# Attention blocks in pairs of heads, with score products alternating between two 64-row halves and maxima negated where they are taken

## The chip, the cores and the metric

The kernel runs on one core of a Trainium2 chip. The metric is the time of one execution on the device in microseconds (us), as the median of several runs; the kernel before takes 3290.98 us (three runs, 3290.24 to 3291.83).

## The reference, cut to what matters

Two transformer-like blocks on a sequence of 1024 rows and a width of 1024, all in float32. The change touches only the attention of the second block, which has 8 heads of 64 channels. It mixes three dilated windows, and each branch normalises itself and is weighted by its softmax denominator:

```
for window, dilation in ((128, 1), (512, 4), (2048, 16)):
    s = einsum(q, k) * HEAD_DIM ** -0.5 - slopes * dist      # causal, masked
    m = max(s); p = exp(s - m); denom = sum(p)
    o = einsum(p, v) / denom;  lse = m + log(denom)
    ...
w = softmax(stack(lses));  o = einsum(w, stack(outs))
```

Because the three weights are the denominators, the mixture equals one causal softmax over all keys, in which a key counts once for each window that reaches it. So the kernel adds to each score a bias (the slope term, the logarithm of that count, and -1e30 where no window reaches) and computes one softmax for each head and each block of 128 queries. Beside it, on the other 512 channels, runs a state-space mixer (S5) of 32 groups of 16 channels.

## The kernel before, in words

The program is written out by hand for five engines, with semaphores between them; nothing reorders it. The big matrix products around the attention are split into high and low parts (lines 125 to 127) and fill most of the span. Between them lies the attention stage, which `att_pe`, `att_act` and `att_dve` write out for TensorE, ScalarE and VectorE.

A *block* n is one head h and one group of 128 queries i; there are 64. Its keys are the first (i + 1) * 128 rows, and its width is counted here in units of 128, k = i + 1, from 1 to 8. Before, n runs through the eight i of a head and then goes to the next head. A block passes through these stations:

- scores (PE, line 1631): one or two products of 64 rows of `QK` into two PSUM banks, chosen by n % 2. Head h uses rows 0 to 63 of the array if h is even, and rows 64 to 127 if it is odd. `scores(n)` waits until the maximum of block n - 2 is taken, since that frees the banks.
- maximum (DVE, line 1728): a custom instruction adds the bias, writes the sum to `sco` and gives its maximum; its second part reads out the accumulator. Line 1733 then multiplies the maximum by -1.
- exponential (ACT, line 1695) with that value as its bias, and the sum of the row as a by-product.
- transposes (PE, line 1641), k of them, into two banks; copy out (ACT, line 1685).
- values (PE, line 1651), k products of 64 columns.
- finish (DVE, lines 1738 and 1741): reciprocal of the sum, and scaling of the result from PSUM.

The engines go in steps n. PE: `scores(n + 2)`, `transposes(n)`, a piece of the state-space mixer, `values(n - 1)`. DVE: `finish(n - 2)`, `maximum(n + 1)`, a piece of the mixer. ACT: exponential of n, copy of n - 1, a piece of the mixer. The mixer's piece is s = n % 8, and it isn't changed. On DVE the pieces are: s0, s2 and s3 short; s4, s5, s6 and s7 long (tables for the next groups, and in s5 and s6 the scan). On PE, s5 waits for the first part of the scan and s7 for the second. GpSimd makes tables and stores at its own pace. The bias of a head (`head_bias`, line 1714) is made from two tables that are built in three cuts during the first head (`bias_dve`, lines 1608 to 1620), and lies in one of two slots, h % 2.

Of the kernel before, what the change touches and what calls it, by code (L numbers as in the profile page):

```python
# [5 lines left out]
P = 128  # L6
S = 1024
D = 1024
NT = S // P
# [34 lines left out]
def program(nc, x, p, stream, cols, rows, gate_mats, pool_mats, inv_count, ssm_g, ssm_bc, x_mid, out):  # L44
# [7 lines left out]
    with ctx:  # L52
# [1512 lines left out]
        def glu_dve(dve):  # L1565
# [32 lines left out]
        at_s, at_m, at_n, at_e, at_tr, at_pt, at_pv, at_r, at_o = (sem(f"at_{s}") for s in (  # L1598
            "s", "m", "n", "e", "tr", "pt", "pv", "r", "o"))
# [22 lines left out]
        def att_pe(pe):  # L1622
            def scores(n):
                h, i = divmod(n, NT)
                rows_ = slice(64 * (h % 2), 64 * (h % 2) + 64)
                W = (i + 1) * P
                if n >= 2:
                    pe.wait_ge(at_m, n - 1)
                for c0 in range(0, W, HALF):
                    w = min(HALF, W - c0)  # L1630
                    last = nc.tensor.matmul(ps[:, 2 * (n % 2) + c0 // HALF, 0:w], QK[rows_, h // 2, i * P:(i + 1) * P],  # L1631
                                            QK[rows_, 4 + h // 2, c0:c0 + w], start=True, stop=True)
                last.then_inc(at_s, 1)

            def transposes(n):
                i = n % NT
                pe.wait_ge(at_e, n + 1)
                if n:
                    pe.wait_ge(at_pt, n)
                for k in range(i + 1):  # L1640
                    last = nc.tensor.transpose(ps[:, 4 + k // 4, (k % 4) * P:(k % 4 + 1) * P],  # L1641
                                               prob[:, n % 2, k * P:(k + 1) * P], ident[:, :])
                last.then_inc(at_tr, 1)

            def values(n):
                h, i = divmod(n, NT)
                pe.wait_ge(at_pt, n + 1)
# [8 lines left out]
            pe.wait_ge(u_out, GT)  # L1656
            scores(0)
            scores(1)
# [19 lines left out]
        def att_act(act):  # L1678
            def rest(n):
                i = n % NT  # L1680
                act.wait_ge(at_tr, n + 1)
# [8 lines left out]
            for n in range(NA):  # L1690
                w = (n % NT + 1) * P
                act.wait_ge(at_n, n + 1)
                if n >= 2:
                    act.wait_ge(at_tr, n - 1)
                nc.scalar.activation(prob[:, n % 2, 0:w], sco[:, n % 2, 0:w], ACT.Exp, bias=nm_[:, n:n + 1],
                                     accum_out=den_[:, n:n + 1]).then_inc(at_e, 1)
# [13 lines left out]
        def att_dve(dve):  # L1710
# [8 lines left out]
            def maximum(n, made):  # L1719
                h, i = divmod(n, NT)  # L1720
                w = (i + 1) * P
# [3 lines left out]
                if n >= 2:  # L1725
# [3 lines left out]
                                               in0=ps[:, b:b + 2, :].rearrange("p a b -> p (a b)")[:, 0:w],  # L1729
                                               in1=bias_h[:, h % 2, S - w:S], scale=1.0, scalar=-3e38, op0=ALU.add,  # L1730
                                               op1=ALU.max, accum_out=mx_[:, n:n + 1]).then_inc(at_m, 1)
                dve.wait_ge(at_m, n + 1)
                nc.vector.tensor_scalar(nm_[:, n:n + 1], mx_[:, n:n + 1], -1.0, None, ALU.mult).then_inc(at_n, 1)

            def finish(n):
                h, i = divmod(n, NT)
                dve.wait_ge(at_e, n + 1)
# [9 lines left out]
            bias_dve(dve, near)  # L1747
            made = [head_bias(0, near)]
            maximum(0, made[0])
            for n in range(NA):  # L1750
                if n % NT == 0:
                    prepare = ssm_prepare_dve(dve, n // NT + 1) if n // NT + 1 < NB else iter(())
                if n == 1 or n == 3:
                    dve.wait_ge(dve_chain, made[0])
                if n >= 2:
                    finish(n - 2)
                if n + 1 < NA:
                    maximum(n + 1, made[(n + 1) // NT])
                if n == 0:
                    dve.wait_ge(io_done, 2)  # L1760
                    bias_dve(dve, middle)
                    made[0] = head_bias(0, middle)
                if n == 2:
                    bias_dve(dve, far)
                    made[0] = head_bias(0, far)
# [459 lines left out]
```

## Time and profile before

| | |
|---|---|
| median of 3 runs | 3290.98 us (3290.24 to 3291.83) |
| profiled execution | 3291.88 us, of it 3290.1 us span |
| PE busy over the span | 3130.1 us (95%) |
| DVE busy | 1519.9 us (46%) |
| ACT busy | 878.3 us (27%) |
| attention stage, from the first maximum to the last finish | about 2098.5 to 2386.0 us |

The span is the time from the first to the last instruction of the profiled execution. Busy shares are means over the whole program, in which the attention stage is less than a tenth; what bounds the stage has to be read from its own stretch. PE's granted clock has two levels, and the profile gives it as a share of 2.4 GHz (1.00 is 2.4 GHz, 0.50 is 1.2 GHz).

### The profile page before, as it was taken

How to read it: one execution, taken by the hardware profiler on the slowest of the kernel's cores; microseconds unless marked ns; L12 is line 12 of the kernel's file. 1: busy time of each engine (PE TensorE's matmuls, PEld its weight loads, DVE VectorE, ACT ScalarE, POOL GpSimd, SP SyncE). 2: the span in 40 equal slices, each digit the busy share in tenths (PEclk: the TensorE clock that was granted, in tenths of full speed). 3: DMA queues.
4: the chain of work that ended last, by engine and by line, in shares of the span. 5: the costliest groups of instructions: out<-in, count | busy, mean ns of one | idle time of the engine just before them, and what ended most of it. 6: DMA issues, size and time to landing. Idle time of an engine off the chain costs nothing.

```text
span 3290.1 us, 36983 instructions
## 1 busy us (share of the span) xinstructions
PE 3130.1 (95%) x14151; PEld 2557.6 (78%) x14151; DVE 1519.9 (46%) x2478; ACT 878.3 (27%) x1323; POOL 172.2 (5%) x372
## 2 busy tenths in 40 slices
PE   7999999999999899999999999899989999999997
PEld 5777888888877678888888778676767788888885
DVE  5654444444454533333333553688745233333335
ACT  5523222221123331111111341145444211111112
POOL 0000000000000000000000001244201000000001
PEclk9999999999999999999999999799989999999998
DMA  3121111111111121111111321000023111111112
GB/s 120 39 80 65 54 51 51 51 45 45 39 51 39 52 77 58 52 38 47 62 45 38 115 90 52 2 5 7 5 77 115 52 51 39 45 61 48 38 51 115
DMA packets 50394, 178.15 MB, mean 54 GB/s; under 512 B 6656, under 2 KB 7424, under 8 KB 50160
## 3 DMA queue, kind: packets, MB, share of 16 engines
q1 hardware_dynamic: 37440, 136.33, 12.3%
q0 software_dynamic: 12848, 40.38, 3.4%
q8 instruction: 70, 1.15, 0.1%
q14 instruction: 36, 0.29, 0.0%
HBM read 158.73 MB, written 16.78 MB: 53 GB/s over the span
## 4 chain that ended last, share of the span: by engine, by line
PE 87%; DVE 8%; ACT 2%; issue 2%; DMA 1%; SPq 0%; DVEq 0%; POOL 0%; ACTq 0%
PE ps L125 27%; PE ps L127 27%; PE ps L126 27%; PE ps L1631 1%; PE ps L261 1%; PE ps L1651 1%; DVE acc L810 1%; DVE sco L1728 1%; DVE region_b L120 1%; DVE acc L176 1%; DVE acc L184 1%; PE ps L1641 0%; ACT region_b L116 0%; PE ps L1454 0%; DMA raw<-stream 0%
## 5 line engine op out<-in xcount | busy, mean ns | idle before, releaser
L125 PE MATMUL ps<-region_a,region_b 128*128 128x512 f32 x1664 | 658.2, 396 | 19.4 <-DVE region_a L220 9.8
L127 PE MATMUL ps<-region_a,region_b 128*128 128x512 f32 x1664 | 650.2, 391 | 0.0
L126 PE MATMUL ps<-region_a,region_b 128*128 128x512 f32 x1664 | 650.2, 391 | 0.0
L810 DVE TENSOR_TENSOR acc<-acc,ps 128x1024 f32<-128x1024 f32 x288 | 351.0, 1220 | 330.3 <-PE ps L127 330.3
L125 PE MATMUL ps<-region_b,region_a 128*128 128x512 f32 x1088 | 431.8, 397 | 17.8 <-DVE region_b L120 10.4
L126 PE MATMUL ps<-region_b,region_a 128*128 128x512 f32 x1088 | 427.9, 393 | 0.0
L127 PE MATMUL ps<-region_b,region_a 128*128 128x512 f32 x1088 | 427.9, 393 | 0.0
L120 DVE TENSOR_TENSOR region_b<-raw,region_b 128x1024 fp32r<-128x1024 f32 x176 | 212.4, 1223 | 390.3 <-ACT region_b L116 390.2
L125 PEld LDWEIGHTS ps<-region_a,region_b 128*128 128x128 f32 x1664 | 314.5, 189 | 87.7 <-issue 10.0
L126 PEld LDWEIGHTS ps<-region_a,region_b 128*128 128x128 f32 x1664 | 314.6, 189 | 65.3 <-issue 1.7
L127 PEld LDWEIGHTS ps<-region_a,region_b 128*128 128x128 f32 x1664 | 314.0, 189 | 66.1
L125 PE MATMUL ps<-region_b 128*128 128x512 f32 x896 | 350.8, 392 | 4.2 <-DVE acc L810 2.8
L127 PE MATMUL ps<-region_b 128*128 128x512 f32 x896 | 348.8, 389 | 0.0
L126 PE MATMUL ps<-region_b 128*128 128x512 f32 x896 | 348.7, 389 | 0.0
L125 PEld LDWEIGHTS ps<-region_b,region_a 128*128 128x128 f32 x1088 | 215.3, 198 | 61.3 <-issue 10.1
L725 ACT ACTIVATE rtmp<-ps 128x512 f32<-128x512 f32 x88 | 52.7, 598 | 735.9 <-PE ps L127 735.9
L127 PEld LDWEIGHTS ps<-region_b,region_a 128*128 128x128 f32 x1088 | 215.1, 198 | 41.1
L126 PEld LDWEIGHTS ps<-region_b,region_a 128*128 128x128 f32 x1088 | 215.3, 198 | 39.4
L116 ACT ACTIVATE region_b<-raw 128x1024 fp32r<-128x1024 f32 x176 | 181.5, 1050 | 161.5 <-DMA raw<-stream 132.0
L120 DVE TENSOR_TENSOR region_a<-raw,region_a 128x1024 fp32r<-128x1024 f32 x74 | 89.5, 1224 | 262.2 <-ACT region_a L116 262.2
L125 PEld LDWEIGHTS ps<-region_b 128*128 128x128 f32 x896 | 168.2, 188 | 40.7 <-DVE acc L810 4.0
L127 PEld LDWEIGHTS ps<-region_b 128*128 128x128 f32 x896 | 168.2, 188 | 35.2
(289 smaller groups left out, 3337.2 us busy)
## 6 DMA issues: line engine op xcount, KB each, us to landing
raw<-stream SPq DMA_DIRECT2D x252, 512.0 KB, 3.2
x_mid<-acc POOLq DMA_DIRECT2D x24, 512.0 KB, 3.1
acc<-x SPq DMA_DIRECT2D x8, 512.0 KB, 8.3
rold<-x POOLq DMA_DIRECT2D x16, 256.0 KB, 3.5
old_a<-x_mid POOLq DMA_DIRECT2D x8, 512.0 KB, 9.5
old_b<-x_mid POOLq DMA_DIRECT2D x8, 512.0 KB, 7.8
out<-acc POOLq DMA_DIRECT2D x8, 512.0 KB, 2.9
old_s<-x_mid POOLq DMA_DIRECT2D x6, 512.0 KB, 5.6
```

Source lines behind the costliest of these rows:

```text
L116: nc.scalar.activation(slot[:, 0, :], raw[:, odd, :], ACT.Copy).then_inc(hi_done, 1)
L120: nc.vector.tensor_tensor(slot[:, 1, :], raw[:, odd, :], slot[:, 0, :].bitcast(f32), ALU.subtract).then_inc(unit_ready, 1)
L125: nc.tensor.matmul(psum, lhs(0), rhs(0), start=first, stop=False)
L126: nc.tensor.matmul(psum, lhs(0), rhs(1), start=False, stop=False)
L127: return nc.tensor.matmul(psum, lhs(1), rhs(0), start=False, stop=last)
L176: nc.vector.scalar_tensor_tensor(out=acc[:, t, :], in0=acc[:, t, :], scalar=rinv_post[:, t:t + 1], in1=gb[:, N.post, :], op0=ALU.mult, op1 ...
L184: nc.vector.scalar_tensor_tensor(out=a, in0=a, scalar=N.factor, in1=N.old(t), op0=ALU.mult, op1=ALU.add).then_inc(N.sem["res"], 1)
L261: last = nc.tensor.transpose(ps[:, 6 + d % 2, t * P:(t + 1) * P], xn[:, t, d * P:(d + 1) * P], ident[:, :])
L725: nc.scalar.activation(rtmp[:, half, :], ps[:, up_bank(c, j, half), :], ACT.Silu).then_inc(F.sem["ge"], 1)
L810: nc.vector.tensor_tensor(acc[:, t, :], acc[:, t, :], src, ALU.add).then_inc(F.sem["de"], 1)
L1631: last = nc.tensor.matmul(ps[:, 2 * (n % 2) + c0 // HALF, 0:w], QK[rows_, h // 2, i * P:(i + 1) * P], QK[rows_, 4 + h // 2, c0:c0 + w], st ...
L1651: last = nc.tensor.matmul(ps[:, 6, 0:HEAD_DIM], probT[:, n % 2, k, :], V[:, k, h * HEAD_DIM:(h + 1) * HEAD_DIM], start=k == 0, stop=k == i)
```

## The change

Blocks are numbered so that two heads, 2p and 2p + 1, run together: n = 16p + 2i + (h % 2). The widths k then go 1, 1, 2, 2, up to 8, 8 in sixteen steps, where before they went 1 to 8 in eight steps. The mixer's pieces stay at n % 8. The scores of both blocks of a pair are issued together, at the even step before, and their products alternate between the two halves of the rows and go to different banks. Before it issues a pair, PE waits for both maxima of the pair before. The instruction for the maximum now multiplies the sum of scores and bias by -1 and takes the minimum, so that its result is the negated maximum; line 1733 is gone, and the exponential uses a scale of -1. The tables of the bias are built at other steps, for two heads at once.

```diff
-        mx_, nm_, den_, rd_ = (stats[:, i, :] for i in range(4))
+        _, nm_, den_, rd_ = (stats[:, i, :] for i in range(4))
+        def block_of(n):
+            pair, r = divmod(n, 2 * NT)
+            return 2 * pair + r % 2, r // 2
...
-            def scores(n):
-                h, i = divmod(n, NT)
-                rows_ = slice(64 * (h % 2), 64 * (h % 2) + 64)
+            def scores_pair(m):
+                h, i = block_of(2 * m)
                 W = (i + 1) * P
-                if n >= 2:
-                    pe.wait_ge(at_m, n - 1)
+                if m:
+                    pe.wait_ge(at_m, 2 * m)
                 for c0 in range(0, W, HALF):
                     w = min(HALF, W - c0)
-                    last = nc.tensor.matmul(ps[:, 2 * (n % 2) + c0 // HALF, 0:w], QK[rows_, h // 2, i * P:(i + 1) * P],
-                                            QK[rows_, 4 + h // 2, c0:c0 + w], start=True, stop=True)
-                last.then_inc(at_s, 1)
+                    for r in range(2):
+                        rows_ = slice(64 * r, 64 * r + 64)
+                        last = nc.tensor.matmul(ps[:, 2 * r + c0 // HALF, 0:w], QK[rows_, h // 2, i * P:(i + 1) * P],
+                                                QK[rows_, 4 + h // 2, c0:c0 + w], start=True, stop=True)
+                        if c0 + w == W:
+                            last.then_inc(at_s, 1)
...
             for n in range(NA):
-                if n + 2 < NA:
-                    scores(n + 2)
+                if n % 2 == 0 and n + 2 < NA:
+                    scores_pair(n // 2 + 1)
...
-                act.wait_ge(at_n, n + 1)
+                act.wait_ge(at_m, n + 1)
...
-                                               in1=bias_h[:, h % 2, S - w:S], scale=1.0, scalar=-3e38, op0=ALU.add,
-                                               op1=ALU.max, accum_out=mx_[:, n:n + 1]).then_inc(at_m, 1)
-                dve.wait_ge(at_m, n + 1)
-                nc.vector.tensor_scalar(nm_[:, n:n + 1], mx_[:, n:n + 1], -1.0, None, ALU.mult).then_inc(at_n, 1)
+                                               in1=bias_h[:, h % 2, S - w:S], scale=-1.0, scalar=3e38, op0=ALU.add,
+                                               op1=ALU.min, accum_out=nm_[:, n:n + 1]).then_inc(at_m, 1)
...
-                if n == 4:
-                    made.append(head_bias(1))
-                if n % NT == NT - 1 and n // NT + 2 < N_HEADS:
-                    made.append(head_bias(n // NT + 2))
+                if n % (2 * NT) >= 2 * NT - 3 and len(made) < N_HEADS and n % (2 * NT) < 2 * NT - 1:
+                    dve.wait_ge(at_m, n + 2)
+                    made.append(head_bias(len(made)))
```

On TensorE, in the second head of the kernel before, step 12 and the beginning of 13 (`qk` are the scores, `prob` the transposes, `ztb`, `zs` and `ub` the mixer, `probT` the values):

```order
L1631 MATMUL ps<-qk 128x512 [waits at_m]
L1631 MATMUL ps<-qk 128x384
L1641 MATMUL ps<-ident,prob 128x128 [waits at_pt,at_e]
L1641 MATMUL ps<-ident,prob 128x128 x4
L1447 MATMUL ps<-ztb 128x128 [waits s5_cp]
L1447 MATMUL ps<-ztb 128x128 x3
L1651 MATMUL ps<-v,probT 128x64 [waits at_o,at_pt]
L1651 MATMUL ps<-v,probT 128x64 x3
L1631 MATMUL ps<-qk 128x512 [waits at_m]
L1631 MATMUL ps<-qk 128x512
```

On TensorE, after the change, steps 10 and 11, with pieces s2 and s3 of the mixer:

```order
L1637 MATMUL ps<-qk 128x512 [waits at_m]
L1637 MATMUL ps<-qk 128x512
L1637 MATMUL ps<-qk 128x384 x2
L1648 MATMUL ps<-ident,prob 128x128 [waits at_pt,at_e]
L1648 MATMUL ps<-ident,prob 128x128 x5
L1442 MATMUL ps<-ident,zs 128x128 [waits s5_cp]
L1442 MATMUL ps<-ident,zs 128x128 x3
L1658 MATMUL ps<-v,probT 128x64 [waits at_o,at_pt]
L1658 MATMUL ps<-v,probT 128x64 x4
L1648 MATMUL ps<-ident,prob 128x128 [waits at_pt,at_e]
L1648 MATMUL ps<-ident,prob 128x128 x5
L1442 MATMUL ps<-ident,ub 128x128 [waits ub_made,s5_cp]
```

Scores no longer come at every step: twice as many come at every second one, ahead of both steps' transposes, and only their first product waits.

On VectorE, in the second head of the kernel before, step 13 (the block of width 7, then the scan's first part, which is piece s5):

```order
L1738 RECIPROCAL stats<-stats 128x1 [waits at_e]
L1741 TENSOR_SCALAR att_o<-ps,stats 128x64 [waits at_pv,at_r]
L1728 ISA sco,stats<-ps,bias_h 128x896 [waits at_e,at_s]
L1728 ISA stats 128x1
L1733 TENSOR_SCALAR stats<-stats 128x1 [waits at_m]
L1373 TENSOR_TENSOR m1b<-ps,cs 128x512 [waits s5_s]
```

On VectorE, after the change, step 13 (the first of the two blocks of width 8, the bias of the next pair's first head, then the scan's first part):

```order
L1742 RECIPROCAL stats<-stats 128x1 [waits at_e]
L1745 TENSOR_SCALAR att_o<-ps,stats 128x64 [waits at_pv,at_r]
L1734 ISA sco,stats<-ps,bias_h 128x1024 [waits at_e,at_s]
L1734 ISA stats 128x1
L1720 SCALAR_TENSOR_TENSOR bias_h<-dist,lmul 128x1024 [waits at_m]
L1373 TENSOR_TENSOR m1b<-ps,cs 128x512 [waits s5_s]
```

The multiplication by -1 is gone, and the bias of a later head has moved ahead of the scan.

## Rows read from the trace of the kernel before

**Rows 1.** Windows: length, busy time and instructions by engine, granted clock, DMA.

```profile
2098.50:2147.20 48.70, 45.53 (x178) 32.20 (x178) 42.18 (x150) 17.90 (x34) 6.98 (x18) 0.60 0.02 4
2215.40:2249.50 34.10, 31.26 (x193) 24.19 (x192) 30.48 (x122) 16.87 (x32) 15.05 (x36) 0.95 0.03 5
2351.90:2386.00 34.10, 31.11 (x204) 24.87 (x202) 14.50 (x51) 16.83 (x31) 4.03 (x8) 0.95 0.03 6
```

**Rows 2.** Timeline of VectorE, third head: start, length, instruction, idle time before.

```profile
2192.61 0.28 DVE L1741 TENSOR_SCALAR att_o<-ps,stats 128x64 f32<-128x64 f32 x1 [0.65 <-PE ps L1651]
2192.81 0.95 DVE L1728 CUSTOM_DVE_ANT_0 sco<-ps,bias_h 128x768 f32<-128x768 f32 x1
...
2193.87 0.28 DVE L1298 TENSOR_TENSOR tmp_v<-z,st 128x128 f32<-128x128 f32 x1
...
2197.86 1.08 DVE L1728 CUSTOM_DVE_ANT_0 sco<-ps,bias_h 128x896 f32<-128x896 f32 x1
2198.86 0.08 DVE L1728 DVE_READ_ACCUMULATOR2_ANT stats<- 128x1 f32 x1
2198.98 0.15 DVE L1733 TENSOR_SCALAR stats<-stats 128x1 f32<-128x1 f32 x1
2199.05 0.68 DVE L1373 TENSOR_TENSOR m1b<-ps,cs 128x512 f32<-128x512 f32 x1
```

**Rows 3.** Timeline of ScalarE, the exponential of the same block.

```profile
2199.17 1.04 ACT L1695 ACTIVATE prob<-sco,stats 128x896 f32<-128x896 f32 x1 [3.02 <-DVE stats L1733]
```

**Rows 4.** Windows of VectorE's pieces s0, s2, s3, s4, s5, s6, bias, s7.

```profile
2182.38:2184.29 1.91, 1.91 (x19) 1.69 (x16) 1.84 (x9) 1.23 (x4) 1.83 (x6) 1.00 0.00 0
2187.90:2189.16 1.26, 1.26 (x13) 1.17 (x11) 1.23 (x4) 1.15 (x4) 1.26 (x2) 1.00 0.00 0
2190.61:2191.79 1.18, 1.18 (x12) 1.01 (x10) 1.11 (x7) 1.06 (x3) 0.98 (x4) 1.00 0.05 14
2193.87:2197.46 3.59, 3.59 (x25) 2.84 (x24) 3.49 (x13) 2.16 (x4) 1.36 (x3) 1.00 0.08 15
2199.05:2202.82 3.77, 3.32 (x27) 2.90 (x26) 3.46 (x29) 1.83 (x3) 0.00 (x0) 1.00 0.01 2
2204.54:2209.77 5.23, 2.94 (x18) 2.29 (x18) 5.06 (x15) 2.04 (x3) 0.00 (x0) 0.89 0.00 0
2210.57:2211.70 1.13, 1.13 (x8) 1.13 (x7) 1.13 (x2) 1.01 (x3) 0.00 (x0) 0.50 0.00 0
2211.70:2215.55 3.85, 3.85 (x29) 3.33 (x28) 3.71 (x14) 3.55 (x4) 2.04 (x5) 0.95 0.00 0
```

**Rows 5.** Chain of waits in order of time: start, length, instructions.

```profile
2181.85 0.98 PE ps L1430 x8
2182.83 1.93 PE ps L1651 x16
2184.76 1.05 PE ps L1631 x2
...
2186.18 0.44 PE ps L1442 x4
...
2188.06 0.48 PE ps L1641 x3
...
2191.88 0.63 PE ps L1651 x6
...
2364.89 0.70 PE ps L1641 x5
2365.59 0.89 PE ps L1447 x8
...
2367.32 1.91 PE ps L1631 x4
```

**Rows 6.** Windows around the scan of the third head.

```profile
2204.00:2208.00 4.00, 2.66 (x19) 1.98 (x18) 3.86 (x10) 2.04 (x3) 0.00 (x0) 1.00 0.00 0
2208.00:2212.00 4.00, 3.05 (x14) 3.08 (x15) 3.86 (x16) 1.31 (x3) 0.00 (x0) 0.58 0.01 4
```

More of the change, by code:

```diff
@@ L1595, in program @@
         stats = at("stats", OFF_B + 31 * KB, [4, N_HEADS * NT])
-        mx_, nm_, den_, rd_ = (stats[:, i, :] for i in range(4))
+        _, nm_, den_, rd_ = (stats[:, i, :] for i in range(4))
         io_done = sem("io_done")
-        at_s, at_m, at_n, at_e, at_tr, at_pt, at_pv, at_r, at_o = (sem(f"at_{s}") for s in (
-            "s", "m", "n", "e", "tr", "pt", "pv", "r", "o"))
+        at_s, at_m, at_e, at_tr, at_pt, at_pv, at_r, at_o = (sem(f"at_{s}") for s in (
+            "s", "m", "e", "tr", "pt", "pv", "r", "o"))
         ot_tr, ot_hi, ot_lo = sem("ot_tr"), sem("ot_hi"), sem("ot_lo")
         NA = N_HEADS * NT
+        def block_of(n):
+            pair, r = divmod(n, 2 * NT)
+            return 2 * pair + r % 2, r // 2
         def bias_dve(dve, cut):
@@ L1656, in att_pe @@
             pe.wait_ge(u_out, GT)
-            scores(0)
-            scores(1)
+            scores_pair(0)
             for n in range(NA):
-                if n + 2 < NA:
-                    scores(n + 2)
+                if n % 2 == 0 and n + 2 < NA:
+                    scores_pair(n // 2 + 1)
                 transposes(n)
@@ L1690, in att_act @@
             for n in range(NA):
-                w = (n % NT + 1) * P
-                act.wait_ge(at_n, n + 1)
+                w = (block_of(n)[1] + 1) * P
+                act.wait_ge(at_m, n + 1)
                 if n >= 2:
                     act.wait_ge(at_tr, n - 1)
-                nc.scalar.activation(prob[:, n % 2, 0:w], sco[:, n % 2, 0:w], ACT.Exp, bias=nm_[:, n:n + 1],
+                nc.scalar.activation(prob[:, n % 2, 0:w], sco[:, n % 2, 0:w], ACT.Exp, bias=nm_[:, n:n + 1], scale=-1.0,
                                      accum_out=den_[:, n:n + 1]).then_inc(at_e, 1)
@@ L1747, in att_dve @@
             bias_dve(dve, near)
-            made = [head_bias(0, near)]
+            made = [head_bias(h, near) for h in range(2)]
             maximum(0, made[0])
@@ L1752, in att_dve @@
                     prepare = ssm_prepare_dve(dve, n // NT + 1) if n // NT + 1 < NB else iter(())
-                if n == 1 or n == 3:
-                    dve.wait_ge(dve_chain, made[0])
+                if n == 3 or n == 7:
+                    dve.wait_ge(dve_chain, made[1])
                 if n >= 2:
@@ L1757, in att_dve @@
                 if n + 1 < NA:
-                    maximum(n + 1, made[(n + 1) // NT])
-                if n == 0:
+                    maximum(n + 1, made[block_of(n + 1)[0]])
+                if n == 1:
                     dve.wait_ge(io_done, 2)
                     bias_dve(dve, middle)
-                    made[0] = head_bias(0, middle)
-                if n == 2:
+                    made = [head_bias(h, middle) for h in range(2)]
+                if n == 4:
                     bias_dve(dve, far)
-                    made[0] = head_bias(0, far)
-                if n == 4:
-                    made.append(head_bias(1))
-                if n % NT == NT - 1 and n // NT + 2 < N_HEADS:
-                    made.append(head_bias(n // NT + 2))
+                    made = [head_bias(h, far) for h in range(2)]
+                if n % (2 * NT) >= 2 * NT - 3 and len(made) < N_HEADS and n % (2 * NT) < 2 * NT - 1:
+                    dve.wait_ge(at_m, n + 2)
+                    made.append(head_bias(len(made)))
                 ssm_step_dve(dve, n, prepare)
```

10 lines of the change are left out of this document (5 added, 5 removed).

## The prediction

> **What bounds the kernel now.** I read first the windows of the attention stage, head by head, since the change touches nothing else. The first head takes longer (48.7 us); from the second on each head takes 34.1 us, with PE busy for 31.3 and DVE for 30.5 [rows 1]. Neither engine is full, so next I read DVE's timeline for what it waits for. Its pieces of the mixer are 1.91 + 1.26 + 1.18 + 3.59 + 3.77 + 5.23 + 3.85 = 20.8 us in a head, and the bias of a later head 1.13 [rows 4]. A maximum with its negation, from its start to the next instruction's, takes 1.06 us at width 6 and 1.19 at width 7 [rows 2], so 0.26 + 0.133k; over k = 1 to 8 that is 6.9 us. A finish is 0.40 (from the end of piece s4 at 2197.46 to the maximum at 2197.86) [rows 2, 4], eight are 3.2. Sum: 32.0 us of the 34.1. The remaining 2 us are waits for PE's values in the light steps; the row with 0.65 us is one [rows 2]. In the steps with s4 to s7 DVE is late, and PE waits: of 8 us around the scan it is busy for 5.7, and its granted clock falls to 0.58 in the second half, which is a stretch at the lower level (1.2 GHz) inside one at 2.4 [rows 6].
>
> So a head is: DVE late in four steps, PE late in the others. PE runs up to two blocks of scores ahead, and this slack couples the two only loosely. The last head shows PE alone: DVE is busy for 14.5 us there and the head still takes about 34 [rows 1].
>
> **Prices of PE's parts**, from one view at full clock [rows 5]: scores 1.05 us at width 4 and 1.91 at width 8, so 0.2 to begin and 0.213k; each product of 512 columns is two MATMULs of 0.43. Transposes 0.48 at 3 and 0.70 at 5: 0.15 + 0.11k. Values 0.63 at 3 and 1.93 at 8: 0.22k or a little more. Mixer: s0 0.98, s1 to s3 0.44 each, s4 and s5 0.89 each (8 instructions), s7 has 24 such instructions, 2.7.
>
> **The change, part by part.**
>
> Negation: 64 instructions leave DVE. The readout starts at 2198.86 and the next instruction after the negation at 2199.05 [rows 2]; without the negation it can follow some 0.06 later, so it saves 0.13 (bounds 0.07 and 0.19). That is 2.1 us in a pair of heads, 8.3 in all, on DVE. The exponential begins 0.31 after the readout [rows 2, 3] and can begin about 0.17 earlier. A maximum now costs 0.13 + 0.133k, and DVE's work for two heads is 61.9 us where it was 64.
>
> Pairing of products: before, adjacent score products use the same rows, so the trace shows no case of two halves side by side. Bounds: each of the extra changes of half costs like a beginning (0.2 us for 12 products more, +2.4 us for two heads), or all passes of one half hide under the other, so that a pair of width k costs 0.2 + 0.213k where two cost 0.4 + 0.427k. A product is two MATMULs that go in order; with alternating products the second of one half lies beside the first of the other, but the two of one half don't lie side by side. So I take a middle: of four passes three remain up to width 4 (0.2 + 0.32k), and five of eight at width 8 (2.35). The Trainium skill, "TensorEngine Tiling (Array Packing)", Key Properties and Theoretical Speedup, says that tiles work in parallel and up to twice as fast, which is the lower of the two bounds. Its PSUM Bottleneck speaks against the change: the evacuation isn't sped up; the rows agree, for DVE holds the heavy steps.
>
> The new wait: PE's scores at an even step n now wait for the maximum of block n + 1, which DVE takes in the same step n, behind `finish(n - 2)`, which waits for `values(n - 2)`, the last thing PE did. Before, PE needed only the maximum of block n, taken a step earlier. So at each of 31 pairs PE stops for at least: values to finish 0.10, finish to maximum 0.20 (2192.61 to 2192.81) [rows 2, 5], the maximum itself 0.133k + 0.08, and some 0.07 to PE. Queued behind the wait are the transposes of n, whose exponential is ready long since, the mixer and the values, for which DVE's next finish waits. Nothing can be carried over from one pair to the next: each round lasts as long as the slower of the two.
>
> A round, from the moment that the second maximum of the pair of width k is taken. PE: 0.07, scores of width k + 1, transposes, piece, values of the block before; then transposes, piece, values; then 0.30 and the maximum. DVE: piece, finish, maximum of the next, piece, finish, maximum; its first finish can't begin before PE's first values are done. The longest path:
> - k = 1 (s0, s1): PE, 0.9 + 0.26 + 0.98 + 1.93, then 0.26 + 0.44 + 0.2, 0.3 + 0.4: 5.7
> - k = 2 (s2, s3): PE to the first values 2.4 (with 0.2 for a copy of the mixer), then DVE 0.3 + 0.4 + 1.18 + 0.4 + 0.4: 5.1
> - k = 3 (s4, s5): DVE, 3.6 + 3.8 + 0.8 + 1.3: 9.5
> - k = 4 (s6, s7): DVE, 5.2 + 3.9 + 0.8 + 1.6: 11.5
> - k = 5 (s0, s1): PE, 2.0 + 0.7 + 1.0 + 0.8, then 0.7 + 0.4 + 1.1, 0.3 + 0.9: 7.9
> - k = 6 (s2, s3): PE, 2.2 + 0.8 + 0.4 + 1.1, then 0.8 + 0.4 + 1.2, 0.3 + 1.1: 8.4
> - k = 7 (s4, s5): PE to the first values 5.5 (2.4 + 0.9 + 0.9 + 1.2); DVE had ended s4 at 3.6 and stood; then DVE 0.3 + 1.2 + bias 1.1 + 3.8 + 0.4 + 1.2: 13.5
> - k = 8 (s6, s7): DVE with the second bias, 1.1 + 5.2 + 3.9 + 0.8 + 0.5: 11.5
>
> Sum 73.1 us for two heads, where it was 68.2: +4.9. The cause is an uneven match: light pieces now fall to the narrow pair and again to the widths 5 and 6, where PE is long and DVE stands (about 3 us each), and DVE can't use that later.
>
> Over the stage: the second and third pair of heads +4.9 each. In the last pair no tables are made in its second half; k = 7 becomes 11.5 and k = 8 about 11, so +2.5. In the first pair the building of the bias (48.7 - 34.1 = 14.6 us more) stays on DVE, but now lies in steps with narrow blocks; PE, at the low clock in much of that window (0.60) [rows 1], has less to do there. I count +3. Sum 15.3.
>
> The clock: after k = 4 PE has finished at about 7.9 of 11.5 and stands 3.6 us, longer than the stretch before the fall of rows 6; after k = 8 it stands twice, 1.2 and 1.4, much as in rows 6. Before, the slow stretch lay under DVE's tables (s7). Now it falls into k = 5 and k = 1, which are PE's. A stretch at half rate costs half of its length; from the window at 0.58, in which some 3.4 us are at the lower level, I take 1.7 for k = 5 and 1 for k = 1, and three pairs of heads to pay it: +8.
>
> The rest of the program is the same, instruction by instruction. Total +23 us: 3291.9 in the profiled execution gives 3314.9; on the median of 3291.0 that is 3314.
>
> **Rivals.**
>
> The halves don't overlap. Then the scores of k + 1 cost 0.2 + 0.427(k + 1), and the rounds come to 6.0, 5.5, 9.6, 11.5, 8.9, 9.6, 14.7, 11.5, sum 77.3. Against 73.1 that is +4.2 in each of four, +17 over the forecast: 3331. For it: no row shows an overlap. Against it: nothing in the program keeps the halves apart, since their banks and rows differ.
>
> The halves overlap fully, and the clock costs nothing. The rounds sum to 71.4, +3.2 for two heads: +3.2 twice, +1 and +1 for the others, so about +8: 3299. For it: the skill's rule and the few low stretches before.
>
> The clock stays low through the light rounds. At half rate PE's parts of k = 1, 2, 5 and 6 (21 us without the stall) cost up to 20 more for two heads; with half of that in each of three pairs, +30 over the forecast's terms without the clock: 3336. For it: the first head at 0.60. Against it: every other head regains 1.00 within 4 us.
>
> Faster: the lock-step costs nothing, because PE's stall lies beside DVE's pieces everywhere. Then DVE's work decides, 61.9 us for two heads, -6.3 each, -25: 3266. It needs PE's rounds k = 1, 2, 5, 6, 7 to be shorter than DVE's; they would have to lose 3 us each at the widths 5 and 6, so my prices of PE would be off by a third. At half of that it's -12: 3279. The negation alone would take this direction.
>
> **How the numbers follow.** Forecast 0.49, of itself 3305 to 3324; no overlap 0.15; full overlap 0.14; low clock 0.11; faster 0.11. A measurement of this kernel tells about 0.2% (6.6 us) from no change. From full overlap I give half to "same" and a little of the forecast's lower edge: same 0.10, faster 0.10, slower 0.80. The range cuts part of the faster case below and of the low clock above: 3287 to 3340.
>
> **What would show it.** Two heads take about 73 us, three times alike, with rounds in which DVE waits about 3 us for values at the widths 5 to 7. PE's longest idle times end at the maximum's readout ahead of each pair of scores. DVE's busy time in the stage falls by some 8 us. Score MATMULs of the two halves start closer together than 0.43 us if they overlap. The granted clock dips after the widths 4 and 8. I'm wrong if two heads take under 68 us, or if PE doesn't wait at the scores; or if the time comes from outside the stage.

## The result, and the profile after

The changed kernel takes 3329.34 us (median of 4, 3326.83 to 3331.08), against 3291.4 of the kernel before on the same chip: a ratio of 1.0114, 95% interval 1.0101 to 1.0126. It is slower by 38 us; the forecast was 23, and the range 3287 to 3340 holds the time. The profiled execution has a span of 3325.0 us, where it was 3290.1 (+34.9); it is the fastest of the four, so its parts add up to some 3 us less than the medians. The attention stage alone has grown by that much, as the windows of its four pairs of heads show (the columns are those of [rows 1]; the same cuts of the kernel before are 82.8, 68.2, 68.4 and 68.1 us long, 287.5 in all):

```profile
2096.71:2190.05 93.34, 65.72 (x368) 52.37 (x368) 69.64 (x257) 35.30 (x66) 21.56 (x53) 0.71 0.02 4
2190.05:2264.21 74.16, 59.22 (x384) 50.03 (x384) 58.11 (x227) 34.78 (x64) 29.02 (x71) 0.84 0.02 5
2264.21:2342.71 78.50, 61.54 (x384) 50.72 (x384) 58.68 (x228) 34.77 (x64) 29.31 (x71) 0.80 0.02 5
2342.71:2418.80 76.09, 59.26 (x396) 48.42 (x396) 41.70 (x157) 34.36 (x62) 16.36 (x37) 0.87 0.02 5
```

The pairs cost 10.5, 6.0, 10.1 and 8.0 us more. From the second pair on neither PE nor DVE is busy for more than about four fifths of it, and the granted clock is 0.80 to 0.87, where [rows 1] has 0.95. So both engines stand in turn. The view of waits over the stage says for what (engine, line, what it waited for: us in total, times, longest):

```profile
DVE att_o L1745 <- PE ps L1658: 70.7, 37, 7.3
PEld ps L1637 <- DVE stats L1734: 64.5, 31, 12.8
PE ps L1637 <- DVE stats L1734: 59.7, 31, 12.6
```

In the kernel before the same view has

```profile
DVE att_o L1741 <- PE ps L1651: 36.8, 33, 4.8
PE ps L1631 <- DVE stats L1728: 11.9, 2, 11.7
```

PE now stops ahead of each of the 31 later pairs of scores, for 48 us more than before: that is the lock-step. DVE waits 34 us more for values; e2 below has nearly the same without the lock-step, so these waits come from the new order of the blocks as well.

The negation is gone as meant. In VectorE's timeline [rows 2] had the readout, the multiplication, and then the mixer's first instruction 0.19 us after the readout; now the mixer starts with the readout:

```profile
2198.21 0.55 DVE L1734 CUSTOM_DVE_ANT_0 sco<-ps,bias_h 128x384 f32<-128x384 f32 x1
2198.68 0.08 DVE L1734 DVE_READ_ACCUMULATOR2_ANT stats<- 128x1 f32 x1
2198.68 0.33 DVE L1298 TENSOR_TENSOR tmp_v<-z,st 128x64 f32<-128x64 f32 x1
```

DVE's busy time fell from 1519.9 to 1509.1 us. And the halves overlap, more than forecast. In the chain of waits, pairs of scores of widths 6, 7 and 8 (each two blocks):

```profile
2221.50 1.56 PE ps L1637 x8
...
2229.15 1.77 PE ps L1637 x8
...
2237.14 1.99 PE ps L1637 x8
```

One block alone took 1.05 at width 4 and 1.91 at width 8 [rows 5]. Two blocks of width 8 now take 1.99, and the three rows give 0.27 + 0.213k for a pair: the second half costs nothing but 0.1 us. By line and form over the stage, the 96 MATMULs of 512 columns show the same: together they keep PE busy for 34.3 us, where it was 57.4. The mean of one record (813 ns; 694 before) doesn't tell the overlap, and it is raised by the lower clock here; in e3, with a stage clock like that of the kernel before (0.88 and 0.89), it is 653 ns:

```profile
L1637 PE MATMUL ps<-qk 64*128 64x512 f32 x96 | 34.3, 813 | 32.4 <-DVE stats L1734 32.4
```

The clock is the rest. Around width 8 of the second pair of heads, windows of 4 us:

```profile
2248.00:2252.00 4.00, 2.41 (x12) 2.00 (x12) 3.41 (x12) 1.19 (x2) 0.00 (x0) 0.50 0.01 2
2252.00:2256.00 4.00, 4.00 (x22) 4.00 (x21) 3.90 (x9) 1.08 (x2) 0.00 (x0) 0.50 0.00 0
2256.00:2260.00 4.00, 4.00 (x20) 4.00 (x21) 3.83 (x20) 2.06 (x4) 0.00 (x0) 0.50 0.00 0
2260.00:2264.00 4.00, 3.90 (x32) 3.76 (x30) 1.61 (x6) 2.40 (x3) 1.68 (x7) 0.89 0.00 0
```

Ahead of them PE had stood for 2.68 us, waiting for the scan. The clock fell in the 3.6 us of work behind that (0.80 in the window 2246 to 2248, 0.50 in the next), and then PE stood for another 1.59 us for the maximum:

```profile
2245.67 1.16 PE L1447 MATMUL ps<-ztb 128*128 128x128 f32 x8 [2.68 <-DVE m1b L1373]
2246.67 2.58 PE L1658 MATMUL ps<-v,probT 128*128 128x64 f32 x14
2250.83 0.58 PE L1637 MATMUL ps<-qk 64*128 64x128 f32 x2 [1.59 <-DVE stats L1734]
```

The clock is then at 1.2 GHz until about 2261, and PE is the late engine there. The chain (start, length) and then DVE's timeline:

```profile
2251.63 1.90 PE ps L1648 x8
2253.53 2.88 PE ps L1658 x14
2256.41 1.71 PE ps L1648 x8
2258.12 0.43 PE ps L1454 x2
```

```profile
2261.52 0.16 DVE L1742 RECIPROCAL stats<-stats 128x1 f32<-128x1 f32 x1
2264.01 0.28 DVE L1745 TENSOR_SCALAR att_o<-ps,stats 128x64 f32<-128x64 f32 x1 [2.33 <-PE ps L1658]
```

DVE is ready at 2261.68 and can begin at 2264.01, when PE is done with the values. Two MATMULs of s7 take 0.22 us at 2.4 GHz and 0.43 here.

Of the runs below, e3 had two disturbed executions among its ten (3985 and 12186 us), which are left out of its median; the texts that were written ahead of later runs quote 3297.8 us, the median with them.

### The profile page after: what moved, and what is told of

It is laid out like the page before. It is cut to its first block, busy times and chain, and to the rows that moved or that the text cites. A ratio compares the mean times of both kernels' runs of the same rounds, so it can differ in the third digit from the quotient of the medians.

```text
span 3325.0 us, 36922 instructions
## 1 busy us (share of the span) xinstructions
PE 3112.9 (94%) x14151; PEld 2559.6 (77%) x14151; DVE 1509.1 (45%) x2416; ACT 881.5 (27%) x1323; POOL 169.8 (5%) x372
## 4 chain that ended last, share of the span: by engine, by line
PE 88%; DVE 8%; ACT 2%; issue 2%; DMA 0%; SPq 0%; DVEq 0%; POOL 0%; ACTq 0%
PE ps L125 27%; PE ps L127 27%; PE ps L126 27%; PE ps L1658 2%; PE ps L261 1%; DVE sco L1734 1%; PE ps L1637 1%; PE ps L1648 1%; DVE acc L810 1%; DVE region_b L120 1%; DVE acc L176 0%; DVE acc L184 0%; PE ps L1447 0%; ACT region_b L116 0%; DVE region_a L220 0%
## 5 line engine op out<-in xcount | busy, mean ns | idle before, releaser
L125 PEld LDWEIGHTS ps<-region_b,region_a 128*128 128x128 f32 x1088 | 215.1, 198 | 60.9 <-issue 10.1
```

Of the source, the lines that this page charges most:

```text
L125: nc.tensor.matmul(psum, lhs(0), rhs(0), start=first, stop=False)
```

## The experiments

All times are medians with the 95% interval of the ratio to the kernel before, which ran beside them (3291.4 to 3292.5 us).

**e1: the negation alone.** The kernel before, with the maximum taken negated.

```diff
-                act.wait_ge(at_n, n + 1)
+                act.wait_ge(at_m, n + 1)
...
-                                               op1=ALU.max, accum_out=mx_[:, n:n + 1]).then_inc(at_m, 1)
-                dve.wait_ge(at_m, n + 1)
-                nc.vector.tensor_scalar(nm_[:, n:n + 1], mx_[:, n:n + 1], -1.0, None, ALU.mult).then_inc(at_n, 1)
+                                               op1=ALU.min, accum_out=nm_[:, n:n + 1]).then_inc(at_m, 1)
```

> The kernel before with the second part of the change alone: the instruction for the maximum gives the negated maximum, the 64 multiplications by -1 are gone, the blocks keep their order and their single scores. Theory (DVE holds the steps with s4 to s7, PE the others): a head loses 0.13 us in each of the 4 to 8 steps in which DVE is late, 34.1 becomes 33.1 to 33.6, so 4 to 8 us in all: 3283 to 3287. Rival (the negation lies in DVE's free time, or PE decides everywhere): 3290 to 3292, heads of 34.1.

Measured: 3288.7 us, ratio 0.9990 (0.9981 to 0.9999). The negation brings 3.5 us, less than half of what it takes off DVE. DVE's waits for values grew instead:

```profile
DVE att_o L1739 <- PE ps L1651: 43.5, 32, 5.0
```

They were 36.8, so 6.7 of the freed time is spent waiting: DVE is late in part of the steps only.

**e2: pairs of heads without the paired scores.** The order of blocks after the change, but each block's scores issued by themselves at each step, with the old wait for block n - 2.

```diff
-                if n % 2 == 0 and n + 2 < NA:
-                    scores_pair(n // 2 + 1)
+                if n + 2 < NA:
+                    scores(n + 2)
```

> The changed kernel with its order of blocks and its negation, but scores issued singly at each step, two blocks ahead, after the maximum of block n alone, as before the change. Nothing of two halves lies side by side any more. Theory (the wait for both maxima ahead of a pair of scores costs more than the overlap gives): PE's idle time ahead of scores (124 us after the change) falls below 30; the scores of two heads cost about 9 us more PE time; rounds by the slower of PE and DVE sum to about 69.5 for two heads plus the low clock, so 3305 to 3318. Rival (the overlap is what keeps the changed kernel from being worse, and the order of the widths against the mixer's pieces is the loss): 3329 or slower, up to 3350.

Measured: 3312.47 us, ratio 1.0054 (1.0039 to 1.0070). Without the lock-step PE waits at the scores only once, for the bias of the first head; the same MATMULs, one after the other, cost 24 us more of PE than in pairs. DVE's waits for values stay at 66.3 us:

```profile
DVE att_o L1744 <- PE ps L1656: 66.3, 38, 7.4
```

```profile
L1636 PE MATMUL ps<-qk 64*128 64x512 f32 x96 | 58.6, 707 | 0.0
L1636 PE MATMUL ps<-qk 64*128 64x256 f32 x32 | 11.3, 437 | 12.4 <-DVE stats L1733 12.4
```

So the order in pairs of heads alone costs about 24 us (3312.5 against 3288.7 of e1), and issuing the scores as pairs at the even step adds 17 more, although it saves PE 39 us of products (92.6 us over all widths here, 53.9 after the change).

**e3: the pairs of scores behind the values.** The changed kernel with one call moved, so that PE does the values of n - 1 before it waits for the maxima.

```diff
-                if n % 2 == 0 and n + 2 < NA:
-                    scores_pair(n // 2 + 1)
                 transposes(n)
                 ssm_step_pe(pe, n)
                 if n:
                     values(n - 1)
+                if n % 2 == 0 and n + 2 < NA:
+                    scores_pair(n // 2 + 1)
```

> The changed kernel with one move: at an even step PE issues the next pair of scores after the transposes, the mixer's piece and the values of that step, not ahead of them. Same wait, same products. Theory (the wait blocks work that is ready): the stall of 0.5 us and the maximum's length at each of 31 pairs lies beside transposes and values; rounds of widths 1, 2, 5, 6 lose about 1 us each, 7 some 0.5 to 1, two heads take 67 to 72 instead of 74 to 78: 3300 to 3315. Rival (the wait only changes sides, DVE now stands for scores at odd steps): within 5 us of 3329.

Measured: 3296.4 us, the median of its eight undisturbed runs (3294.0 to 3300.4), ratio 1.0014 (1.0004 to 1.0024). The place of the wait is worth 33 of the 38 us. The waits at the scores have gone, and DVE's for values are back where they were:

```profile
L1637 PE MATMUL ps<-qk 64*128 64x512 f32 x96 | 27.0, 653 | 0.0
```

```profile
DVE att_o L1745 <- PE ps L1658: 34.3, 30, 5.1
```

**e4: the clock kept up.** The changed kernel, with products that nobody reads issued ahead of those scores and transposes at which PE would stand (16 products of 384 columns in 16 steps).

```diff
+            def filler(n, count):
+                if n and count:
+                    pe.wait_ge(at_pt, n)
+                    for _ in range(count):
+                        nc.tensor.matmul(ps[:, 4, 0:HALF - P], QK[:, 0, 0:P], QK[:, 4, 0:HALF - P], start=True, stop=True)
...
+                filler(n, {6: 4, 8: 4, 14: 2, 0: 1}.get(n % 16, 0))
                 if n % 2 == 0 and n + 2 < NA:
                     scores_pair(n // 2 + 1)
+                filler(n, {5: 1, 13: 3, 15: 1}.get(n % 16, 0))
                 transposes(n)
```

> The changed kernel with products that nobody reads, of 384 columns on all 128 rows (about 0.64 us each at full clock), put on PE where the trace after the change shows it standing for 1 to 4 us: four ahead of the scores at steps 6 and 8 of each sixteen, two at 14, one at 0, and one, three and one ahead of the transposes at steps 5, 13 and 15. 16 in each pair of heads, some 10 us of PE time added. Theory of the clock (PE at 1.2 GHz after its stalls is what the prediction sized too small): the granted clock of the stage rises towards 1.00, the last round of two heads goes from 14.7 to about 12, the fifth from 10.3 to 7.5 where it was that long, two heads take 71 to 73, so 3310 to 3320. Rival (the clock is only a symptom under waits that last anyway): the added work shows, 3329 to 3340.

Measured: 3316.59 us, ratio 1.0071 (1.0055 to 1.0086): 12.8 us less than the changed kernel, with work added. The second pair of heads:

```profile
2191.00:2262.76 71.76, 60.31 (x416) 46.30 (x416) 58.85 (x227) 34.88 (x65) 30.32 (x71) 1.00 0.03 5
```

At 2.4 GHz throughout it takes 71.8 us (the third 71.8 too), where the changed kernel had 74.2 and 78.5. Its first pair of heads takes 90.1, at a granted clock that is still 0.79.

**e5: the halves not side by side.** The changed kernel, with all products of one half first, then a product of 16 columns over all rows, then the other half.

```diff
-                for c0 in range(0, W, HALF):
-                    w = min(HALF, W - c0)
-                    for r in range(2):
-                        rows_ = slice(64 * r, 64 * r + 64)
+                for r in range(2):
+                    rows_ = slice(64 * r, 64 * r + 64)
+                    if r:
+                        nc.tensor.matmul(ps[:, 2, 0:16], QK[:, 0, 0:P], QK[:, 4, 0:16], start=True, stop=True)
+                    for c0 in range(0, W, HALF):
+                        w = min(HALF, W - c0)
```

> The changed kernel with the same wait and the same pairs, but all products of the lower half first, then one product of 16 columns on all 128 rows (its result is overwritten), then all of the upper half, so that no two halves lie side by side. Theory (alternating halves run fully beside each other; the trace after the change has 1.77 us for eight MATMULs of a pair of width 7 where two single blocks of before have 3.4): a pair of width 7 takes about 3.4 to 3.5 us again, two heads get about 6 us longer, 3329 becomes 3345 to 3357. Rival (the halves overlap little, and the shorter span of the scores in the trace is how MATMUL ends are modelled): within 5 us of 3329.

Measured: 3444.95 us, ratio 1.0463 (1.0447 to 1.0479), far above what either theory gave. The same stretch of the stage, of e5 and of the changed kernel:

```profile
2100.00:2380.00 280.00, 238.05 (x990) 177.60 (x990) 157.38 (x611) 88.91 (x170) 72.30 (x177) 0.63 0.02 3
```

```profile
2100.00:2380.00 280.00, 211.49 (x1295) 171.90 (x1293) 212.57 (x814) 119.74 (x224) 91.60 (x218) 0.79 0.02 5
```

PE is busier and does less: the granted clock is 0.63, mostly the level of 1.2 GHz. The cost of the products can't be told from the cost of the clock in this run.

**e6: the negation with other places for the tables.** e1, with one part of the next groups' tables on DVE in nearly each step. The numbers are how many parts DVE makes in the steps s0 to s7.

```diff
-        S5_PIECES = (1, 0, 0, 1, 2, 2, 1, 2)
+        S5_PIECES = (1, 1, 1, 2, 1, 1, 1, 1)
```

> The kernel before with the negation taken in the maximum (as in the first experiment, 3288.7 us), and VectorE's nine pieces that prepare the mixer spread 1, 1, 1, 2, 1, 1, 1, 1 over the eight steps of a head in place of 1, 0, 0, 1, 2, 2, 1, 2. Theory (a head is the sum over steps of the slower engine, and DVE stands in the light steps while it is late in s4 to s7): some 2 us a head move from late steps into DVE's idle time, 33.4 becomes 31.5 to 32.5, so 8 to 15 us: 3273 to 3281. Rival (PE alone needs the time, as in the last head): 3287 to 3290.

Measured: 3298.09 us, ratio 1.0018 (1.0009 to 1.0027): 9 us slower than e1, where the theory had it faster. The part now in s1 is six instructions, and each lasts as long as one of GpSimd's beside it. DVE's timeline, then GpSimd's:

```profile
2183.76 0.65 DVE L1299 TENSOR_TENSOR tmp_v<-zs,st 128x64 f32<-128x64 f32 x1
2184.33 0.65 DVE L1300 TENSOR_TENSOR tmp_v<-zs,st 128x64 f32<-128x64 f32 x1
```

```profile
2183.71 0.61 POOL L1299 TENSOR_TENSOR tmp_p<-vs,st 128x256 f32<-128x256 f32 x1
2184.29 0.61 POOL L1300 TENSOR_TENSOR tmp_p<-vs,st 128x256 f32<-128x256 f32 x1
```

The six take 3.6 us in this place (2183.48 to 2187.04).

**e7: e3 with the same places.**

```diff
-        S5_PIECES = (1, 0, 0, 1, 2, 2, 1, 2)
+        S5_PIECES = (1, 1, 1, 2, 1, 1, 1, 1)
```

> The changed kernel with the scores issued after the values (third experiment, 3297.8 us) and the same spreading 1, 1, 1, 2, 1, 1, 1, 1 of the mixer's pieces. Theory (what is left of the loss is the match of light pieces with PE's long rounds and of heavy pieces with DVE's): rounds 3, 4, 7 and 8 lose 1.5 to 2.5 us each and the light ones grow by less, two heads go from 69 or 70 to 63 to 66: 3275 to 3288. Rival (the rounds are bound by the chain scores, maximum, exponential, transposes and not by the pieces): 3294 to 3300.

Measured: 3306.98 us, ratio 1.0044 (1.0031 to 1.0058), 11 us slower than e3. Moving the parts costs about as much in both orders of blocks. Here too the time is lost where s1 falls: in the second pair of heads the rounds of the widths 1 and 5 (s0 and s1) take 7.7 and 10.3 us, 4.2 and 5.9 in e3, and the heavy round of width 7 gains 3.5. That GpSimd is the cause in this run wasn't looked at.

**e8: the negation, no part in s1.** e1 with

```diff
-        S5_PIECES = (1, 0, 0, 1, 2, 2, 1, 2)
+        S5_PIECES = (1, 0, 1, 2, 1, 2, 1, 1)
```

> The kernel before with the negation in the maximum and the mixer's pieces spread 1, 0, 1, 2, 1, 2, 1, 1. Step s1 gets none, where the sixth experiment lost: there six VectorE instructions of 64 columns took 0.35 to 0.78 us beside GpSimd's tables, 3.4 us together, where the same piece takes 1.2 at s3. Theory (VectorE's short instructions are slowed while GpSimd works in s0 and s1): away from it the spreading gains, a head takes 31.8 to 33 instead of 33.4, 3276 to 3286. Rival (light steps have no free time at all for more of it): 3288 to 3298.

Measured: 3281.52 us, ratio 0.9971 (0.9959 to 0.9983), 17 us faster than e6, from which it differs by one part fewer in s1 and one more in s5; the parts between move by a step. The six instructions that e6 has in s1 stand in s2 here, beside the end of GpSimd's tables, and take 1.4 us (2181.23 to 2182.65) in place of 3.6. Four of them run at 0.20 each within one of GpSimd's, which is the one held: it has 1.24 us in place of the 0.73 to 0.76 of its like. The fifth then lasts until about its end:

```profile
2181.50 0.20 DVE L1300 TENSOR_TENSOR tmp_v<-zs,st 128x64 f32<-128x64 f32 x1
...
2181.88 0.64 DVE L1302 TENSOR_TENSOR z<-tmp_v 128x64 f32<-128x64 f32 x1
```

```profile
2181.19 1.24 POOL L1303 TENSOR_TENSOR vs<-tmp_p 128x256 f32<-128x256 f32 x1
```

So the two seem to take turns. From the maximum of width 3 to that of width 4, e6 takes 1.9 to 2.6 us more than e8 in each of six heads and 1.1 in the first, 15 us in all; that is the price of the place. Beside it, two heads of e6 lose another 2.8 us each between the maxima of widths 6 and 7, with the granted clock down. The second head, of e6 and of e8:

```profile
2139.06:2176.03 36.97, 34.34 (x195) 26.07 (x194) 31.38 (x116) 17.08 (x32) 15.99 (x35) 0.86 0.03 5
2139.01:2170.95 31.94, 29.54 (x195) 22.66 (x194) 29.72 (x116) 16.95 (x32) 15.66 (x35) 1.00 0.03 6
```

Other steps give back some of it; the profiled spans differ by 13 us. The Trainium skill, "GPSIMD Engine Reference", Key points, says that GpSimd shares its SBUF interfaces with VectorE, with contention for instructions of two SBUF inputs. These have two, and the trace agrees; its price here is up to a factor of three.

**e9: the negation, with two parts in s4 and s7.** e8 with

```diff
-        S5_PIECES = (1, 0, 1, 2, 1, 2, 1, 1)
+        S5_PIECES = (1, 0, 1, 1, 2, 1, 1, 2)
```

> As the run before it, but 1, 0, 1, 1, 2, 1, 1, 2: step s3 gets the third piece (1.4 us), not the third and the fourth (3.6). Theory: s3 now stays within PE's time of that step (about 3 us), s5 loses 1.4, a head takes 32 to 33: 3277 to 3286. Rival as there: 3288 or more.

Measured: 3291.42 us, ratio 0.9990 (0.9981 to 0.9999); the eleven runs fall into two groups, five from 3283.4 to 3286.8 and six from 3291.4 to 3292.6. In the profiled one, of the second group, the second head takes 41.7 us and each of the next five 32.2 to 33.1. For some 20 us of that head PE is busy all the time and the granted clock stays down, then it comes back:

```profile
2148.00:2152.00 4.00, 4.00 (x12) 2.34 (x12) 1.44 (x7) 1.53 (x4) 3.84 (x8) 0.52 0.00 0
...
2164.00:2168.00 4.00, 4.00 (x13) 2.49 (x12) 3.45 (x21) 1.75 (x4) 0.00 (x0) 0.50 0.00 0
2168.00:2172.00 4.00, 4.00 (x22) 2.69 (x21) 2.23 (x8) 1.35 (x2) 0.00 (x0) 0.92 0.00 0
```

e8 has no such stretch. The same window of it, with twice the MATMULs:

```profile
2148.00:2152.00 4.00, 4.00 (x23) 2.72 (x22) 3.86 (x15) 1.82 (x5) 3.77 (x9) 1.00 0.00 0
```

This head's excess is 9.5 us (41.7 - 32.2), and the medians of the two groups are 6.5 apart. That the faster group lacks the stretch wasn't seen, since only one run has a trace. But its runs have a mean granted clock of 0.977, like those of e8, and the others 0.974: 0.003 of 3290 us is some 10 us of full clock, or 20 us at half (an estimate from rounded figures), which is about the stretch.

**e10: e3, with a few products that nobody reads ahead of the transposes, and one part moved in every second group of the mixer.**

```diff
-        S5_PIECES = (1, 0, 0, 1, 2, 2, 1, 2)
+        S5_PIECES = ((1, 0, 0, 1, 2, 2, 1, 2), (1, 0, 1, 1, 1, 2, 1, 2))
...
+                filler(n, {6: 2, 8: 2}.get(n % 16, 0))
+                filler(n, {5: 1, 13: 2, 15: 1}.get(n % 16, 0))
                 transposes(n)
```

> The third experiment (scores after the values) with three smaller things: products that nobody reads at fewer places (two ahead of steps 6 and 8, one, two and one ahead of the transposes at 5, 13 and 15), and, in the second half of each pair of heads alone, the mixer's pieces 1, 0, 1, 1, 1, 2, 1, 2. Theory: rounds 7 and 8, 13.3 to 13.8 and 12.5 to 13.4, lose 1 to 1.5 each from the pieces and the clock; two heads take 67 instead of 69 or 70: 3286 to 3294 against 3297.8. Rival (neither is on the path there): 3296 to 3302.

Measured: 3294.54 us, ratio 1.0005 (0.9996 to 1.0014): 2 us under e3, no change against the kernel before. Its pairs of heads take 83.3, 68.9 and 67.6 us, so the paired order was brought to where the old order stood, and with these edits not below it.

**e11: e5 with the products of e4**, the same `filler` with the same counts.

```diff
+                filler(n, {6: 4, 8: 4, 14: 2, 0: 1}.get(n % 16, 0))
                 if n % 2 == 0 and n + 2 < NA:
                     scores_pair(n // 2 + 1)
+                filler(n, {5: 1, 13: 3, 15: 1}.get(n % 16, 0))
```

> The fifth experiment (halves apart, 3444.9 us) with the products of the fourth that nobody reads. The fifth cost 115 us against 16 to 28 expected. Theory (6 us for two heads are the lost overlap, the rest is the low clock, which holds for most of the stage there: 0.50 to 0.6 in most stretches of 20 us): with fillers the clock stays at 1.00 as in the fourth and the time falls to 3335 to 3350, 20 to 30 over the fourth's 3316.6. Rival (a product on other rows between the halves costs much by itself, about 3.5 us at each pair): it stays above 3400.

Measured: 3391.25 us, ratio 1.0301 (1.0286 to 1.0317). Some 54 us of e5's excess over the changed kernel was the clock's. The stage is still not at full clock:

```profile
2100.00:2380.00 280.00, 246.65 (x1174) 174.94 (x1174) 170.31 (x646) 98.37 (x185) 79.49 (x185) 0.80 0.02 4
```

A pair of width 6 at full clock in PE's timeline:

```profile
2246.82 1.55 PE L1639 MATMUL ps<-qk 64*128 64x512 f32 x4
2248.30 0.40 PE L1636 MATMUL ps<-qk 128*128 128x16 f32 x2
2248.63 1.55 PE L1639 MATMUL ps<-qk 64*128 64x512 f32 x4
2250.11 0.66 PE L1649 MATMUL ps<-ident,prob 128*128 128x128 f32 x4
```

From the first start to the transposes it is 3.29 us, of which 0.33 the small product; 2.96 for the scores. Side by side, in the changed kernel, the same distance is 1.49 (2221.50 to 2222.99). This is the overlap measured on the same blocks, in the same place of the program and at full clock in both: 1.47 us at width 6.

**e12: e8 with one product that nobody reads, in step s7, ahead of the transposes.** No pairs of heads.

```diff
+                filler(n, 1 if n % NT == 7 else 0)
                 transposes(n)
```

> The eighth experiment (the kernel before with the negation in the maximum and pieces 1, 0, 1, 2, 1, 2, 1, 1; 3281.5 us) with one product of 384 columns that nobody reads ahead of the transposes of each head's last step, where PE stands 1.0 us for the scan behind them. Theory (what is left of the clock's falls costs there): a head that takes 33 to 33.6 there takes 32 like the others, and the granted clock stays at 1.00: 3276 to 3280. Rival (PE's falls lie under VectorE's work in this order): 3281 to 3285, the added product shows a little.

Measured: 3279.26 us, ratio 0.9962 (0.9949 to 0.9976). It is the fastest of all, 13 us under the kernel before (3292.53 beside it) and 50 under the changed one. Against e8 it gains 2.3 us, with intervals that overlap, and not where it was expected: heads of nearly 33 us are still there, and in the profiles the last head is the one that is shorter (36.3 us, 39.0 in e8).

## Why the prediction came out as it did

**Lock-step: right in kind, and the largest term.** The prediction said that PE would stop at each of 31 pairs and that nothing could be carried from one to the next. e3 takes that away by moving one call and gets 33 us back, part of it clock that no longer falls; e2 does it in another way and gets 17 back, in spite of losing the overlap. The forecast of two heads at full clock was 73.1 us; e4 shows 71.8, twice.

**Overlap of the halves: wrong size, in the kernel's favour.** The sum took "a middle" because a product is two MATMULs that go in order, 0.2 + 0.32k up to width 4 and 2.35 us at width 8. The chain shows 0.27 + 0.213k, 1.99 at width 8; so of the two bounds the lower one holds. With that bound the prediction's rounds sum to 71.4, which is e4's 71.8. The remark that the two MATMULs of one half can't lie side by side was true and had no bearing, since the other half always had one to put beside each. The Trainium skill's rule that is quoted there ("TensorEngine Tiling (Array Packing)", Key Properties) agrees with the trace.

**The ends of the stage: the first pair of heads was priced too low.** The prediction gave the first pair +3 and the last +2.5, each before the clock; they cost 10.5 and 8.0 with it. In the first, the far tables of the bias stand in DVE's queue ahead of the scan, and PE has nothing to do meanwhile:

```profile
2128.31 1.01 PE L1447 MATMUL ps<-ztb 128*128 128x128 f32 x3 [9.26 <-DVE m1b L1373]
```

It then works at 1.2 GHz; the round of k = 3 takes 18.3 us, where later ones take 9.4. I had counted the narrow blocks as a relief for PE, but they are a lack of cover. With the clock kept up later on, this pair still takes 90.1 us in e4, 7.3 more than before. In the last pair most of what was missing is the clock. PE has s7 behind the scan, at 1.2 GHz (5.5 us instead of 2.7), with only the last two blocks of values behind it. From the chain:

```profile
2408.37 0.77 PE ps L1454 x2
...
2413.83 2.11 PE ps L1658 x16
```

**The clock: the term that failed most, in size and in place.** The prediction let each of three pairs of heads pay 1.7 us at k = 5 and 1 at k = 1, +8 in all. e4 got 12.8 us back, net of what its added products cost. The rounds, from the moment at which the second maximum of the pair of width k is taken (its readout) to the next one's, and for k = 8 of the last pair to the last finish, were:

| k | forecast, full clock | second pair of heads | third | last | e4, second and third |
|---|---|---|---|---|---|
| 1 | 5.7 | 5.6 | 5.6 | 5.6 | 5.6 |
| 2 | 5.1 | 4.9 | 4.9 | 4.8 | 4.8 |
| 3 | 9.5 | 9.4 | 9.4 | 9.4 | 9.4 |
| 4 | 11.5 | 11.3 | 11.4 | 11.2 | 11.5 |
| 5 | 7.9 | 7.7 | 10.4 | 10.5 | 7.7 |
| 6 | 8.4 | 8.0 | 8.0 | 7.9 | 8.0 |
| 7 | 13.5 (last 11.5) | 13.7 | 15.1 | 11.5 | 13.2 |
| 8 | 11.5 (last 11) | 13.7 | 13.7 | 14.9 | 11.6 |

The forecast's rounds at full clock were good: e4 has each of them within 0.4 us. What they left out is the clock. k = 1 pays nothing. k = 5 pays 2.8 us in the third pair of heads and 2.9 in the last, k = 7 up to 1.8, and k = 8 pays 2.1 in the second and the third pair and 2.9 in the last (where e4 has 12.0). I had taken k = 8 as DVE's round, where a slow PE is covered ("the slow stretch lay under DVE's tables"). But the round has two blocks of transposes and one of values near their widest, 6.5 us of PE at 1.2 GHz (1.90 + 2.88 + 1.71), and then s7 at 0.43 us a pair of MATMULs. Round by round against e4, the low clock costs 2.4 us in the second pair of heads, 6.7 in the third, 5.8 in the last (k = 5 and 8) and 3.2 in the first, where e4 itself isn't at full clock: 18 us at least, where 8 stood.

**The sum.** Over the four pairs of heads the forecast was 23.3 and the profile has 34.6. The clock: 18.1 where 8 stood, +10.1. The first pair without it: 7.3 (e4) where 3 was forecast, +4.3. The second and third at full clock: 6.9 (e4) where 9.8 were forecast, -2.9. The last without the clock: 2.2 where 2.5 stood, -0.3. That is, to a rounding, the 11.3 us that were missing. The range held because it had been drawn wide, toward a rival with a low clock.

**The negation: right on DVE, too much on the path.** It saved 0.19 us a block on DVE's timeline, the upper of the bounds. e1 shows 3.5 us in the program. The rival that it alone would go faster held; the rival that it would carry the whole change down to 3266 didn't.

**The rivals.** No overlap would have given 3331, close to the 3329 measured, but that is luck: its cause, halves that don't overlap, is excluded by the trace and by e11. Of the low clock through the light rounds only k = 5 is seen. Full overlap was true, but not with a clock that costs nothing.

**What stays open.** e11 is 75 us above e4, 18.7 for two heads. The products kept apart account for about 11 of them (0.13 + 0.213k for the second block and 0.33 for the small product, summed over the eight widths). The rest lies in a stage with a clock of 0.80, and its causes weren't taken apart. In the second pair of heads e11 is longer than e4 by 3.4, 3.6 and 2.3 us at the widths 1 to 3, by 1.8 at 5, by 6.9 and 5.5 at 6 and 7, and by nothing at 4 and 8. Why the clock stays down in e9 with PE never idle is not known either. The stretch holds the same products as the other heads, scores for more than half of its time, and PE had stood for only 0.96 us (up to 2146.14) ahead of it.

## What to carry to other kernels

Where an engine waits for another, ask first what stands behind the wait on its queue: here one call moved behind the values was worth 33 of the 38 us lost, although score products at twice the speed had saved PE 39 us of work. An instruction's price holds for its place: moved beside GpSimd's work, 0.22 us on DVE became 0.65. And price the first turn of a loop by itself, since there the cover can be missing. A stall that costs nothing by itself can be paid some microseconds later, at half the clock, in a stretch that had been covered; price the covered stretch at 1.2 GHz too.

## What the runs showed of the hardware that was not expected

- Products on rows 0 to 63 and rows 64 to 127 run fully beside each other when they alternate, in float32 too: two blocks of width 8 in 1.99 us, one alone in 1.91. The record of one MATMUL doesn't tell the overlap (653 ns on average in e3, 694 in the kernel before, at stage clocks of 0.88 and 0.89); the busy time of the engine (27.0 and 57.4 us) and the distance of starts do.
- A DVE operation on two tensors of 128x64 takes 0.20 to 0.22 us, and 0.65 to 0.78 when it falls between GpSimd's; in one place GpSimd was held instead (1.24 us for 0.73).
- The granted clock stayed at 0.50 for some 20 us while PE was busy for 4.00 of 4.00 us (e9), and 16 products without use in each pair of heads, ahead of waits of 1 to 4 us, kept it at 1.00 in the second and third pair and saved 12.8 us in all (e4).
